# Identity turns at two seams of a one-core decoder step, a fourth early step in the MLP, and six pieces moved behind decode's last group

## The chip, the cores and the metric

The kernel runs on one core of a Trainium2 chip. The metric is the device time in microseconds of one execution. Before the change three runs took 1118.14, 1119.84 and 1120.73 us; the median is 1119.84.

## The reference

One layer of a hybrid decoder is applied to a prompt of 512 tokens and to 64 new tokens (8 sequences of 8) that have 2048 cached positions each. Width is 1024, all values are 32-bit floats.

```
h  = rmsnorm(x) ;  z = h @ w_in                 # q, k, v of two branches, gates ga, gm
att = block-sparse attention (top 3 of the blocks of 256 positions, and the own block)
ml  = chunked matrix memory with running-max stabiliser, 4 heads of 128
u   = sigmoid(ga) * (att @ w_attn_br) + sigmoid(gm) * (ml @ w_mlstm_br)
x   = x + rmsnorm(u @ w_out)
y   = x + rmsnorm(square(relu(rmsnorm(x) @ w_up)) @ w_down)      # w_up 1024 x 4096
```

For the new tokens the attention reads all cached keys of their sequence (for block means and scores) and the cached values, through a page table: 64 MB in pages of 128 positions.

## The kernel before

Every engine has one instruction stream, written out by hand; semaphores order them, and each engine works strictly in its own order. The stages are: first norm and turn of x, projection with the matrix memory beside it, prompt attention, decode attention, merge, MLP.

**Matmuls.** 32-bit products are made of three matmuls with reduced operands: each operand is split in a high part (ScalarE, `w_high`, L336) and a low part (VectorE, `w_low`, L347). One step is 128 rows of a weight chunk of 512 columns; it is loaded by SP into one of four slots, split, and used by TensorE. A slot can be filled again when TensorE has used it. In `features_chunk` (L497) a step is 24 matmuls: eight PSUM banks, three matmuls each; even banks hold the first half (288) of the 576 tokens, odd banks the second. With `early` the first `EARLY` = 3 steps do their even banks first, then a callback, then their odd banks, and then the other steps follow. So TensorE can work while the last token tiles aren't ready.

**First seam.** `first_pe` waits for the identity matrix (semaphore `masked`, made by POOL), then turns the normed tiles 0 to 3 with eight transposes each (`first_turn`, L571). ScalarE copies the high part out (L596), VectorE the low part (L607). Tile 4 (the 64 new tokens) is turned inside the first `features_chunk`, after its first step.

**Second seam.** After the merge's last matmuls (`kept_tiles`, L435 and L442), VectorE forms the new x (L2377), its norm (L552), and TensorE turns each tile (`mixed_turn`, L2226). Tile 3's turn stands at the end of `pe_merge`. The MLP's first chunk then does three steps' even banks, `last_turn` (tile 4's turn, and a wait until banks 1, 3, 5 and 7 are free), and goes on. ScalarE and VectorE split three steps (`AHEAD` = 3) at e == 2 in `act_merge` and `dve_merge`, the others in `act_mlp` and `dve_mlp`.

**Decode.** The work on the cache is 32 groups of four pages, taken in slots. In slot s TensorE forms the scores of group s-1 (L1928), turns the keys of group s (four times four transposes, L1919), turns the probabilities of group s-6 (L1944), and multiplies them with the values (L1960). Keys arrive on SP's queue in a ring of two groups, values on POOL's queue in another. At two places in each slot, ahead of the last two key turns and behind the values, TensorE takes half pieces of other work: gates (L890) and branches (L906). `pieces_in(s)` says how many whole pieces a slot holds. A piece is 12 matmuls; branch pieces are emptied by VectorE (L2185) in its next slot. In every fourth slot (s % 4 == 0) VectorE chooses the blocks of a sequence (`choose`), and ScalarE's exponentials of that sequence start in the slot after. Slots 32 to 39 have no new keys; they finish the values. All pieces together are 80 and their order is fixed; how many stand in each slot decides also in which slot the weights for them are fetched and split (`steps_in`, `fetched_in`).

Of the kernel before, what the change touches and what calls it, by code (L numbers as in the profile page):

```python
# [15 lines left out]
P = 128  # L16
D = 1024
KT = D // P
T = 512
PT = T // P  # L20
# [19 lines left out]
AHEAD = 3  # L40
# [54 lines left out]
def moba_mlstm_step(  # L95
# [57 lines left out]
    h2T = stacked("h2T", "R2", True)  # L153
# [60 lines left out]
    w_hi, w_lo, _ = pair("w", [P, NSLOT, CH], "RW")  # L214
# [4 lines left out]
    ident = sb("ident", [P, P], F32, "RC")  # L219
# [60 lines left out]
    def sem(name):  # L280
        if name not in names:
            names[name] = stack.enter_context(nc.semaphore(name))
        return names[name]
# [191 lines left out]

    EARLY = 3

    def features_chunk(eng, n, right, kt, nts=4, early=()):  # L480

        w = (w_hi, w_lo)
        slots = []
        parts = [(k, h) for h in range(2) for k in range(EARLY)] if early else []
        parts += [(k, None) for k in range(len(parts) // 2, kt)]
        for k, half in parts:
            if k == len(slots):
                slots.append(take_step(eng, n))
            j = slots[k]
            for b in range(2 * nts):  # L490
                i, h = b // 2, b % 2
                if half not in (None, h):
                    continue
                if k == 0:
                    fill(eng, n, b)
                for c, a in THREE:
                    mm = eng.matmul(ps[:, b, 0:HALFT], w[a][:, j, i * P:(i + 1) * P],  # L497
                                    right[c][:, k, h * HALFT:(h + 1) * HALFT],
                                    start=(k == 0 and (c, a) == THREE[0]),
                                    stop=(k == kt - 1 and (c, a) == THREE[-1]))  # L500
                if k == kt - 1 and b < 2 * nts - 1:
                    filled(mm, n, b)
            if half != 0:
                mm.then_inc(sem(f"w_used{j}"), 1)
            if half == 0 and k in early:
                early[k]()
# [39 lines left out]
    def norm_tile(eng, tag, e, t, src, dst, gain):  # L546
# [5 lines left out]
        eng.scalar_tensor_tensor(out=dst[0:r, t, :], in0=src[0:r, t, :], scalar=rinv[0:r, t:t + 1],  # L552
                                 in1=gain[0:r, :], op0=ALU.mult, op1=ALU.mult).then_inc(sem("normed"), 1)

    def first_pe(eng, n):

        eng.wait_ge(sem("masked"), 1)
        for t in range(PT):
            first_turn(eng, n, t)

    def first_bank(t, j):
        return (0, 1, 2, 3, 4, 5, 7, 1, 3, 5)[2 * t + j]
# [375 lines left out]
    def pieces_in(s):  # L938

        if s < VALS:  # L940
            return 2
        if s < ALL_GROUPS:
            return 2 if s % 4 == 0 else 1
        return (2, 1, 1, 2, 1, 1, 2, 0)[s - ALL_GROUPS]

    def pieces_at(g):
        return 2 - g % 2 if g < A_SLOTS else pieces_in(g - A_SLOTS)
# [1282 lines left out]
    def act_merge(eng, n):  # L2230
        for f in range(KT):
            w_high(eng, n)
            for h in range(2):
                skip(n, h, h == 1)
                eng.wait_ge(sem("u_sum"), 2 * f + h + 1)
                eng.activation(uT[0][:, f, h * HALFT:(h + 1) * HALFT], u_at(f, h), ACT.Copy, scale=0.5)\
                   .then_inc(sem("u_high"), 1)
        for _ in range(KT - AHEAD):
            w_high(eng, n)
        for k in range(KT):  # L2240
            w_high_kept(eng, n, wo_res, k)

        def squares(t, c, e):
            drain(eng, n, t, t == PT and c == 0, KT)
            if t < PT:
                eng.wait_ge(sem("mix_sq"), c * PT + e)
                eng.activation(junk2[:, 0:CH], ps[:, t, :], ACT.Square, accum_out=(sq0, sq1)[c][:, t:t + 1])\
                   .then_inc(sem("mix_sq"), 1)
            else:
                eng.activation(wide[0:NS, PT, c * CH:(c + 1) * CH], ps[LOW, PT, :], ACT.Copy)\  # L2250
                   .then_inc(sem("low_part"), 1)
                n["low_part"].add()
            n[f"free{t}"].add()

        def rms_of_mixed(e):
            t = ORDER[e]
            r = rows(t)
            squares(t, 1, e)
            if t < PT:
                eng.wait_ge(sem("mix_sqe"), 1)  # L2260
            else:
                eng.wait_ge(sem(f"free{PT}"), n[f"free{PT}"].value())
                eng.activation(junk2[0:NS, :], wide[0:NS, PT, :], ACT.Square, accum_out=sq1[0:NS, PT:TILES])\
                   .then_inc(sem("mix_sq"), 1)
            eng.wait_ge(sem("mix_sq"), PT + e + 1)
            eng.activation(rms[0:r, t:t + 1], sq1[0:r, t:t + 1], ACT.Sqrt,
                           bias=sqe[:, t:t + 1] if t < PT else eps[0:r, :], scale=1.0 / D).then_inc(sem("mix_rms"), 1)

        def rms_of_x(e):
            t = ORDER[e]  # L2270
            r = rows(t)
            eng.wait_ge(sem("x_sum"), e + 1)
            eng.activation(junk2[0:r, :], x[0:r, t, :], ACT.Square, accum_out=ssq[0:r, t:t + 1])\
               .then_inc(sem("squares"), 1)
            eng.wait_ge(sem("squares"), TILES + e + 1)
            eng.wait_ge(sem("mix_rinv"), e + 1)
            eng.activation(rms[0:r, t:t + 1], ssq[0:r, t:t + 1], ACT.Sqrt, bias=eps[0:r, :], scale=1.0 / D)\
               .then_inc(sem("rms"), 1)

        for t in range(TILES):  # L2280
            squares(t, 0, t)
        eng.wait_ge(sem("mix_sq"), PT)
        eng.activation(sqe[:, 0:PT], sq0[:, 0:PT], ACT.Identity, bias=eps[:, :], scale=1.0 / D)\
           .then_inc(sem("mix_sqe"), 1)
        for e in range(TILES):
            if e >= 1:
                rms_of_x(e - 1)
            if e >= 2:
                mixed_high(eng, n, e - 2)
            rms_of_mixed(e)  # L2290
            if e == 2:
                for _ in range(AHEAD):
                    w_high(eng, n)
        mixed_high(eng, n, TILES - 2)
        rms_of_x(TILES - 1)
        mixed_high(eng, n, TILES - 1)
# [25 lines left out]
    def dve_merge(eng, n):  # L2322
# [63 lines left out]
        for e in range(TILES):  # L2386
            if e >= 1:
                norm_tile(eng, 1, e - 1, ORDER[e - 1], x, xn, g2B)
            if e >= 2:
                mixed_low(eng, n, e - 2)  # L2390
            added(e)
            if e == 2:
                for _ in range(AHEAD):
                    w_low(eng, n)
        mixed_low(eng, n, TILES - 2)
        norm_tile(eng, 1, TILES - 1, ORDER[TILES - 1], x, xn, g2B)
# [17 lines left out]

    def pe_mlp(eng, n):
        def body(i, last):
            features_chunk(eng, n, h2T, KT, early={EARLY - 1: last_turn} if i == 0 else ())
            features_chunk(eng, n, h2T, KT)
            tokens_chunk(eng, n, hid, KT, lambda k: eng.wait_ge(sem("hid_low"), i * 16 + 2 * k + 2))
            if last:  # L2420
                for _ in kept_tiles(eng, n, hid, wd_res):
                    pass
            else:
                tokens_chunk(eng, n, hid, KT)

        def last_turn():
            mixed_turn(eng, n, TILES - 1)
            for b in (1, 3, 5, 7):
                eng.wait_ge(sem(f"free{b}"), n[f"free{b}"].value())


        for b, later in ((5, 1), (6, 0), (7, 0)):
            eng.wait_ge(sem(f"free{b}"), n[f"free{b}"].value() - later)
        mlp_passes(body)

    def act_mlp(eng, n):
        def body(i, last):
            for c in range(2):
                for _ in range(KT):
                    w_high(eng, n)  # L2440
                for b in range(9):
                    if b < 8:
                        drain(eng, n, b, b == 7)
                        eng.wait_ge(sem("hid_low"), i * 16 + 8 * c)
                        drained(eng.activation(rl[:, b, :], ps[:, b, 0:HALFT], ACT.Relu), n, b)
                    if b >= 1:
                        u = b - 1
                        eng.wait_ge(sem("hid_sq"), i * 16 + 8 * c + u + 1)
                        k = 4 * c + u // 2
                        eng.activation(hid[0][:, k, (u % 2) * HALFT:(u % 2 + 1) * HALFT], rl[:, u, :], ACT.Copy)\  # L2450
                           .then_inc(sem("hid_high"), 1)
            if last:
                return
            for c in range(2):
                for _ in range(KT):
                    w_high(eng, n)
                for t in range(TILES):
                    skip(n, t, t == TILES - 1)
# [27 lines left out]
    def dve_mlp(eng, n):  # L2486
        def body(i, last):
            for c in range(2):
                for _ in range(KT):
                    w_low(eng, n)  # L2490
                for b in range(9):
                    if b < 8:
# [181 lines left out]
```

## Time and profile before

| what | value |
|---|---|
| median of three runs | 1119.84 us |
| profiled execution | 1118.83 us |
| its span, first to last instruction | 1117.2 us |
| TensorE busy | 1066.3 us (95%) |
| VectorE / ScalarE / POOL busy | 563.8 / 449.5 / 126.6 us |
| mean granted TensorE clock | 0.989 |

PE is TensorE's matmul side, PEld its weight loads, DVE is VectorE, ACT ScalarE, POOL GpSimd, SP the engine that issues loads; ACTq is ScalarE's queue. Transposes appear as MATMUL with `ident`. L571 is line 571 of the kernel; a line can be that of a helper. "[1.96 <-DVE xn L552]" says that the engine was idle for 1.96 us before the instruction and what released it.

### The profile page before, as it was taken

What the parts mean: (1) busy time and instruction counts of PE and PEld (TensorE: products, weight loads), DVE (VectorE), ACT (ScalarE), POOL (GpSimd) and SP (SyncE); (2) the same over time, 40 slices, a digit from 0 to 9 for tenths busy, and PEclk for the clock granted to TensorE, in tenths of its full rate; (3) what the DMA queues carried; (4) which work ended last, traced back from release to release, by engine and by line L of the source; (5) the groups of instructions that cost most, each with busy time, mean ns of one, the idle gap of its engine ahead of it and who ended that gap; (6) DMA issues with size and microseconds to landing.
All of it is one profiled execution on the core that took longest, in us unless ns stands there. A gap on an engine that the chain in (4) does not pass through costs nothing.

```text
span 1117.2 us, 20695 instructions
## 1 busy us (share of the span) xinstructions
PE 1066.3 (95%) x7593; PEld 910.2 (81%) x7593; DVE 563.8 (50%) x1227; ACT 449.5 (40%) x1023; POOL 126.6 (11%) x227
## 2 busy tenths in 40 slices
PE   4999999999999999999988998999999999999997
PEld 4977877887777777767768886998899899889985
DVE  5254534545675655655644747443344334433456
ACT  5253233324554555555543355342144113322441
POOL 4003110221001033323331100100000000000000
PEclk8999999999999999999999999999999999999999
DMA  6432216234136799989974440223222222222222
GB/s 214 117 86 57 67 48 142 57 85 124 48 96 188 202 326 309 322 308 339 321 218 132 150 134 29 95 76 94 84 77 86 85 76 86 80 81 85 77 85 85
DMA packets 93716, 150.02 MB, mean 134 GB/s; under 512 B 9377, under 2 KB 39590, under 8 KB 93622
## 3 DMA queue, kind: packets, MB, share of 16 engines
q1 hardware_dynamic: 75040, 103.83, 30.6%
q0 software_dynamic: 11968, 39.85, 10.6%
q10 hardware_dynamic: 6614, 5.06, 1.6%
q8 instruction: 61, 1.00, 0.4%
q14 instruction: 33, 0.27, 0.1%
HBM read 141.62 MB, written 7.10 MB: 133 GB/s over the span
## 4 chain that ended last, share of the span: by engine, by line
PE 78%; DVE 9%; issue 4%; ACT 3%; DMA 3%; SPq 1%; POOLq 1%; ACTq 1%; POOL 0%; DVEq 0%
PE ps L462 27%; PE ps L497 19%; PE ps L890 7%; PE ps L470 4%; PE ps L1919 4%; PE ps L906 3%; PE ps L435 2%; DMA kring<-in_cache_k_dram 2%; PE ps L1928 1%; PE ps L1960 1%; DVE xn L552 1%; PE ps L1054 1%; PE ps L1074 1%; PE ps L1064 1%; ACT sP L2036 1%
## 5 line engine op out<-in xcount | busy, mean ns | idle before, releaser
L347 DVE TENSOR_TENSOR w<-w,w 128x512 fp32r<-128x512 f32 (+1 forms) x240 | 168.0, 706 | 305.6 <-ACT w L336 301.0
L336 ACT ACTIVATE w<-w 128x512 fp32r<-128x512 f32 (+1 forms) x240 | 145.2, 613 | 337.7 <-PE ps L470 172.4
L497 PE MATMUL ps<-h2T,w 128*128 128x288 f32 x1536 | 210.0, 297 | 4.3 <-DVE wide L2529 1.7
L497 PEld LDWEIGHTS ps<-h2T,w 128*128 128x128 f32 x1536 | 207.1, 189 | 7.2 <-DVE wide L2529 2.4
L462 PE MATMUL ps<-w,hid 128*128 128x512 f32 x672 | 161.6, 389 | 0.0
L462 PEld LDWEIGHTS ps<-w,hid 128*128 128x128 f32 x672 | 125.9, 188 | 26.0
L462 PE MATMUL ps<-w,hT 128*128 128x512 f32 x576 | 145.3, 401 | 1.4 <-ACT ri L811 1.4
L462 PEld LDWEIGHTS ps<-w,hT 128*128 128x128 f32 x576 | 106.0, 190 | 26.6 <-issue 4.9
L890 PE MATMUL ps<-hT,w 128*128 128x288 f32 x768 | 124.2, 305 | 0.0
L890 PEld LDWEIGHTS ps<-hT,w 128*128 128x128 f32 x768 | 104.7, 188 | 11.3 <-issue 10.6
L1886 POOL DMA_DIRECT2D vring<-in_cache_v_dram x128 | 68.8, 538 | 180.1 <-issue 180.1
L1919 PEld LDWEIGHTS ps<-ident,kring 128*128 128x128 f32 x512 | 56.6, 140 | 36.5 <-DMA kring<-in_cache_k_dram 18.5
L2090 DVE COPY kT<-ps 128x512 f32<-128x512 f32 x64 | 44.1, 689 | 79.3 <-PE ps L1919 79.1
L1919 PE MATMUL ps<-ident,kring 128*128 128x128 f32 x512 | 68.5, 277 | 8.4 <-DMA kring<-in_cache_k_dram 4.6
L2020 ACT ACTIVATE kT<-ps 128x512 f32<-128x512 f32 x64 | 38.2, 597 | 37.8 <-PE ps L1919 37.7
L2036 ACT ACTIVATE sP<-sS,sbias 128x256 f32<-128x256 f32 x64 | 31.7, 498 | 26.2 <-DVE sbias L2122 26.2
L1960 PE MATMUL ps<-vring,sPT 128*32 128x128 f32 x1024 | 34.8, 276 | 6.4 <-DMA vring<-in_cache_v_dram 6.4
L497 PE MATMUL ps<-hT,w 128*128 128x288 f32 x240 | 35.0, 310 | 3.5 <-DVE w L347 3.5
L497 PEld LDWEIGHTS ps<-hT,w 128*128 128x128 f32 x240 | 34.5, 201 | 3.8 <-issue 3.7
L1960 PEld LDWEIGHTS ps<-vring,sPT 128*32 128x32 f32 x1024 | 26.0, 109 | 12.0 <-DMA vring<-in_cache_v_dram 7.1
L470 PE MATMUL ps<-w,hid 128*128 128x512 f32 x112 | 34.5, 389 | 0.0
L1928 PE MATMUL ps<-kT,qb 128*32 128x512 f32 x256 | 34.1, 605 | 0.0
(354 smaller groups left out, 1279.1 us busy)
## 6 DMA issues: line engine op xcount, KB each, us to landing
kring<-in_cache_k_dram SPq DMA_DIRECT2D x128, 256.0 KB, 4.1
vring<-in_cache_v_dram POOLq DMA_DIRECT2D x128, 256.0 KB, 4.5
w<-in_w_in_dram SPq DMA_DIRECT2D x88, 256.0 KB, 2.9
w<-in_w_up_dram SPq DMA_DIRECT2D x64, 256.0 KB, 2.8
w<-in_w_down_dram SPq DMA_DIRECT2D x64, 256.0 KB, 2.8
w<-in_w_out_dram SPq DMA_DIRECT2D x16, 256.0 KB, 3.0
x<-in_x_prompt_dram SPq DMA_DIRECT2D x4, 512.0 KB, 6.9
out_dram<-sC ACTq DMA_DIRECT2D x1, 2048.0 KB
```

The costliest lines, as they stand in the source:

```text
L336: eng.activation(spread(w_hi, n, j, width), together(w32, n, j, width), ACT.Copy)\
L347: eng.tensor_tensor(spread(w_lo, n, j, width), together(w32, n, j, width), spread(w_hi, n, j, width).bitcast(F32), ALU.subtract).then_inc( ...
L462: mm = eng.matmul(ps[:, t, :], left[a][:, k, prompt_cols(t)], w[b][:, j, :], start=(k == 0 and (a, b) == THREE[0]), stop=(k == kt - 1 and ...
L470: mm = eng.matmul(ps[:, PT, :], left[2][:, k, T:NT + NS], w[b][:, j, :], start=(k == 0 and b == 0), stop=(k == kt - 1 and b == 1))
L497: mm = eng.matmul(ps[:, b, 0:HALFT], w[a][:, j, i * P:(i + 1) * P], right[c][:, k, h * HALFT:(h + 1) * HALFT], start=(k == 0 and (c, a) == ...
L890: mm = eng.matmul(ps[:, h, 0:HALFT], w[a][:, slots[part], (k % 4) * P:(k % 4 + 1) * P], hT[c][:, k, h * HALFT:(h + 1) * HALFT], start=(k = ...
L1886: eng.dma_start(ring[:, 4 * (g % 2) + j, :], flat[bass.ds(page, 1), :, :].rearrange("a p n -> (a p) n"))\
L1919: mm = eng.transpose(ps[:, 2 + h % 2, j * P:(j + 1) * P], kring[:, (m % 2) * 4 + j, h * P:(h + 1) * P], ident[:, :])
L1928: mm = eng.matmul(ps[32 * h:32 * h + 32, 4, :], qb[:, (m // GROUPS) % 2, h, :], kT[:, h, :], start=True, stop=True)
L1960: mm = eng.matmul(ps[32 * h:32 * h + 32, 6, 0:P], sPT[m % 2][:, j, 32 * h:32 * h + 32], vring[:, 4 * (m % 2) + j, h * P:(h + 1) * P], star ...
L2036: eng.activation(sP[m % 2][:, c], sS[:, g * CH:(g + 1) * CH][:, c], ACT.Exp, bias=sbias[:, 2 * g + k:2 * g + k + 1], scale=SC, accum_out=s ...
L2090: eng.tensor_copy(kT[:, h, :], ps[:, 3, :]).then_inc(sem("p_kT_dve"), 1)
```

## The change

Five things are done. A helper `keep_busy` issues transposes of the identity into a PSUM bank that nobody reads at that time. `first_pe` calls it with 28 turns before tile 0, 5 after tiles 0, 1 and 2, and 16 after tile 3. The MLP's first chunk has four early steps instead of three, and ScalarE and VectorE split the fourth with the three others. `last_turn` gets 8 identity turns before tile 4's turn, and 12 between the waits for its banks. In decode the slots 8, 12, ... 28 hold one piece instead of two, and the slots from 32 on hold (3,2,2,3,2,2,2,0) instead of (2,1,1,2,1,1,2,0).

```diff
-    EARLY = 3
+    EARLY, EARLY_UP = 3, 4
...
-        parts = [(k, h) for h in range(2) for k in range(EARLY)] if early else []
+        parts = [(k, h) for h in range(2) for k in range(max(early) + 1)] if early else []
...
+    def keep_busy(eng, b, times):
+
+        for _ in range(times):
+            eng.transpose(ps[:, b, 0:P], ident[:, :], ident[:, :])
+
     def first_pe(eng, n):
 
         eng.wait_ge(sem("masked"), 1)
+        keep_busy(eng, 6, 28)
         for t in range(PT):
             first_turn(eng, n, t)
+            keep_busy(eng, 6, 5 if t < PT - 1 else 16)
...
         if s < ALL_GROUPS:
-            return 2 if s % 4 == 0 else 1
-        return (2, 1, 1, 2, 1, 1, 2, 0)[s - ALL_GROUPS]
+            return 1
+        return (3, 2, 2, 3, 2, 2, 2, 0)[s - ALL_GROUPS]
...
             if e == 2:
-                for _ in range(AHEAD):
+                for _ in range(EARLY_UP):
                     w_high(eng, n)
...
             if e == 2:
-                for _ in range(AHEAD):
+                for _ in range(EARLY_UP):
                     w_low(eng, n)
...
-            features_chunk(eng, n, h2T, KT, early={EARLY - 1: last_turn} if i == 0 else ())
+            features_chunk(eng, n, h2T, KT, early={EARLY_UP - 1: last_turn} if i == 0 else ())
...
         def last_turn():
+            keep_busy(eng, 7, 8)
             mixed_turn(eng, n, TILES - 1)
-            for b in (1, 3, 5, 7):
+            for b in (5, 1):
+                eng.wait_ge(sem(f"free{b}"), n[f"free{b}"].value())
+            keep_busy(eng, 1, 12)
+            for b in (3, 7):
                 eng.wait_ge(sem(f"free{b}"), n[f"free{b}"].value())
...
-                for _ in range(KT):
+                for _ in range(KT - (EARLY_UP - AHEAD if i == c == 0 else 0)):
                     w_high(eng, n)
...
-                for _ in range(KT):
+                for _ in range(KT - (EARLY_UP - AHEAD if i == c == 0 else 0)):
                     w_low(eng, n)
```

## Rows read from the trace of the kernel before

**Rows 1.** The page, part 1: busy time, share of the span, instructions.
```profile
PE 1066.3 (95%) x7593; PEld 910.2 (81%) x7593; DVE 563.8 (50%) x1227; ACT 449.5 (40%) x1023; POOL 126.6 (11%) x227
```

**Rows 2.** Windows: stretch and length; busy (instructions) by engine; clock, DMA, GB/s.
```profile
20.84:27.67 6.83, 6.83 (x33) 6.44 (x32) 2.87 (x7) 0.77 (x3) 1.47 (x2) 0.50 0.85 253
...
567.70:604.85 37.15, 29.91 (x365) 25.93 (x365) 13.21 (x38) 11.44 (x32) 10.75 (x20) 0.95 0.63 181
696.68:703.50 6.82, 4.94 (x24) 4.78 (x25) 2.19 (x6) 1.79 (x4) 4.90 (x2) 0.50 0.19 77
398.13:567.70 169.57, 163.93 (x1909) 127.07 (x1909) 99.93 (x251) 94.82 (x244) 51.59 (x96) 1.00 0.93 318
```

**Rows 3.** Timeline of PE, 0 to 75 us: start, length, instruction, idle before.
```profile
15.58 1.09 PE L571 MATMUL ps<-ident,xn 128*128 128x128 f32 x8 [0.86 <-DVE xn L552]
20.15 2.62 PE L497 MATMUL ps<-hT,w 128*128 128x288 f32 x12 [3.47 <-DVE w L347]
...
23.75 32.39 PE L497 MATMUL ps<-hT,w 128*128 128x288 f32 x228
```

**Rows 4.** Line 571's turns, 11.0 to 11.5 and 16.0 to 16.5 us: min/median/max ns.
```profile
L571 PE MATMUL ps<-ident,xn x4: 421/421/421, 10.8 to 11.4; 128*128 128x128 f32 x4
...
L571 PE MATMUL ps<-ident,xn x7: 272/272/273, 15.7 to 16.4; 128*128 128x128 f32 x7
```

**Rows 5.** Timeline of POOL, ACT's queue and DVE, 0 to 32 us.
```profile
3.68 0.29 POOL L646 TENSOR_SCALAR_AFFINE_SELECT ident<-ident 128x128 f32<-128x128 f32 x1 [0.23 <-POOL vm L624]
...
24.80 5.18 ACTq L2607 DMA_DIRECT2D snn<-in_state_n_dram  x1
...
30.82 1.29 DVE L347 TENSOR_TENSOR w<-w,w 128x512 fp32r<-128x512 f32 x2 [5.56 <-ACT w L336]
```

**Rows 6.** Timeline of PE, 655 to 726 us.
```profile
687.80 1.09 PE L2226 MATMUL ps<-ident,xn 128*128 128x128 f32 x8 [1.96 <-DVE xn L552]
689.15 4.97 PE L497 MATMUL ps<-h2T,w 128*128 128x288 f32 x36 [0.26 <-issue]
696.86 1.11 PE L2226 MATMUL ps<-ident,xn 64*128 64x64 f32 x8 [2.74 <-DVE xn L552]
699.68 26.55 PE L497 MATMUL ps<-h2T,w 128*128 128x288 f32 x180 [1.70 <-DVE h2T L2315]
```

**Rows 7.** Timelines of DVE and POOL, 655 to 730 us.
```profile
678.25 1.89 DVE L347 TENSOR_TENSOR w<-w,w 128x512 fp32r<-128x512 f32 x3
...
683.43 1.28 DVE L2377 SCALAR_TENSOR_TENSOR x<-wide,rinv,x 128x1024 f32<-128x1024 f32 x1
...
698.46 4.37 POOL L2592 MEMSET wide<- 128x5120 f32 x1 [0.82 <-ACT h2T L2303]
```

**Rows 8.** Timeline of PE, decode slots 24 to 28.
```profile
512.00 1.07 PE L1928 MATMUL ps<-kT,qb 128*32 128x512 f32 x8
...
520.07 1.06 PE L1928 MATMUL ps<-kT,qb 128*32 128x512 f32 x8
...
523.76 1.09 PE L1919 MATMUL ps<-ident,kring 128*128 128x128 f32 x8 [0.36 <-ACT kT L2020]
...
539.61 1.06 PE L1928 MATMUL ps<-kT,qb 128*32 128x512 f32 x8
```

**Rows 9.** Timelines of DVE and ACT, 505 to 525 us.
```profile
517.45 0.69 DVE L2090 COPY kT<-ps 128x512 f32<-128x512 f32 x1 [1.32 <-PE ps L1919]
...
521.07 0.51 ACT L2036 ACTIVATE sP<-sS,sbias 128x256 f32<-128x256 f32 x1 [3.00 <-DVE sbias L2122]
```

**Rows 10.** Waits of PE, 567.7 to 604.9 us: total, times, longest.
```profile
PE ps L1960 <- DMA vring<-in_cache_v_dram: 6.4, 3, 3.6
```

**Rows 11.** Timeline of PE behind the last group.
```profile
567.70 1.06 PE L1928 MATMUL ps<-kT,qb 128*32 128x512 f32 x8
...
574.99 1.03 PE L906 MATMUL ps<-mlT,w 128*128 128x288 f32 x6 [0.81 <-DVE sg L2185]
...
600.60 4.25 PE L906 MATMUL ps<-mlT,w 128*128 128x288 f32 x30
```

## The prediction

> **What bounds the kernel now.** I read the page first (busy shares, then the clock line), then the windows, then the order of instructions in the three places that the change touches. TensorE is busy 95% of the span [rows 1], so time comes only from its idle stretches and from stretches at the lower of its two clock levels (1.2 GHz against 2.4).
>
> At the first seam TensorE turns tile 3 at 15.58 and then idles 3.47 us until VectorE has split the first weights; the first matmuls start at 20.15 [rows 3], and soon after the granted clock is 0.50 for 6.83 us [rows 2]. From 23.75 on, 228 matmuls run with no idle in 32.39 us [rows 3]. At 0.1333 us each (3.2 us a step of 24) they need 30.4; the missing 2.0 is half of the slow time from 23.75 to 27.67. So the dip is paid in full. At the second seam it is the same after two idle stretches: 1.96 us ahead of tile 3's turn is followed by no fall, 2.74 us ahead of tile 4's turn is; TensorE then goes on at 699.68, and the clock is 0.50 until 703.50 [rows 2, 6]. In decode, slots 8 to 31 take 169.57 us, with TensorE busy 163.93 and the DMA engines at 0.93 [rows 2]: the two are nearly balanced. After the last group TensorE has gaps again, 6.4 us of them on V pages [rows 10].
>
> **First seam.** The first idle-filling turns wait only for the identity, made at 3.97 [rows 5]. Turns are 421 ns from issue to end at the start and 272 ns by 16 us, the row's figure at full clock [rows 4]; eight take 1.09 us at full clock [rows 3], so about 0.117 each, and I take 0.213 each at half. 28 of them from 4.0 end at 9.97 at the latest, where tile 0's turn starts at 9.90 now: no cost, or 0.1. Tiles 1 to 3 are given by VectorE, and 8 turns plus 5 identity turns (1.5 us at full clock) fit between them. Behind tile 3's turn (16.67) 16 more take about 1.8, to 18.3. The idle stretch before 20.15 shrinks from 3.47 to about 1.9, as long as the 1.96 that was followed by no fall. I take it that the clock holds: 6.83 / 2 = **3.4 us** gained. Late next: step 3's high part stands on ScalarE behind a DMA issue of 5.18 us (24.80 to 29.98), and its low part is done at about 31.5 [rows 5]. That issue starts about 0.9 earlier (tile 4's turn runs at full clock), so the low part comes at 30.5; TensorE wants it at 20.15 + 3 x 1.6 + 0.6 + 4.8 = 30.35. It costs 0.2. **Seam 1: -3.2** (bounds: -3.4; and +3.3, all added turns at half clock, below).
>
> The Trainium skill, TensorE: Matmul & The Clock Gate, Part 4, speaks against this: transposes don't count as PE-busy in the same way, and the full clock doesn't engage for them. The trace disagrees: from 9.90 to 14 the engine did nothing but turns, and within them they went from 421 to 272 ns [rows 4]. By the rule both seams' clock gains would be nothing.
>
> **Second seam.** Four steps' first halves instead of three: 12 matmuls, 1.6 us, move from behind the second-half point into the wait for tile 4. What is added ahead of it: a fourth split. On ScalarE 0.6 us in an idle stretch, hidden. On VectorE three low parts take 1.89 [rows 7] in a row of work without gaps (it still has none before 683.43 [rows 7]), so the fourth delays everything behind it by 0.6: the sums, norms and turns of tiles 3 and 4. Tile 3's turn goes from 687.80 to 688.4, and its idle stretch from 1.96 to 2.56. The 48 matmuls start at 689.75 and end at 696.3 (36 took 4.97 [rows 6]); 8 identity turns end at 697.2, before tile 4 is ready at 697.4. The turn takes about half of its 1.11 [rows 6], so the copies start some 0.3 earlier; 12 turns more (1.3 us) end at 699.3. Second halves then start at 699.68 + 0.6 - 0.3 = 700.0. Behind it 144 matmuls instead of 156: -1.6. The clock: from 699.68 to 703.50 half is lost, 1.9. Weights: step 4's low part waits for POOL's clearing of the sum, done at 702.8 [rows 7], and is wanted at 706.4: hidden. **Seam 2: +0.3 - 1.6 - 1.9 = -3.2** (bounds: -3.8 without the delay; +0.4 with all turns at half clock).
>
> **Decode.** A piece is 12 matmuls: 30 take 4.09 us before the next group starts [rows 11], so 1.64. Six leave slots 8, 12, ... 28; each had half ahead of the last key turns, half behind the values. Four slots now take 539.61 - 512.00 = 27.61, the first 8.07 [rows 8]. But slot 1 of each four has a wait for ScalarE's kT copy (0.36 at 523.76 [rows 8]). Behind it is a chain: last key turn of slot 0, VectorE's copy at 517.45, the choice of blocks, then ScalarE's exponentials at 521.07 after 3.00 idle [rows 9], then kT. It is about 6.4 us long and doesn't shrink. Only the half piece ahead of its start shortens the period; the half behind it turns into wait, 0.36 to about 1.2. So 6 x 0.82 = 4.9 us leave the slots, not 9.8. Of 5.64 us idle in these slots [rows 2] six kT waits make 2.2, so K pages cost some 3.5 now; with DMA at 0.93 [rows 2] there is a little room, and I take 0.6 of new waits: **-4.3**.
>
> After the last group (567.70 to 604.85, 37.15 us) TensorE is busy 29.91 at a clock of 0.95 [rows 2]: about 1.7 of the busy time is the clock. Work at full clock is 28.2; six pieces make 38.0. V pages no longer hold it up (they do now for 6.4 us, since POOL issues them at a fixed pace). But slot 32's third piece needs bank 0, which VectorE empties only after its choice of blocks, seen at 574.99 [rows 11]; TensorE gets there 0.81 (the wait now) and 0.47 (the four turns ahead of it) earlier, at 573.7, and waits 1.3: 39.3 in all, **+2.2**. The page tables, POOL's and SP's queues get no new instruction. **Decode: -4.3 + 2.2 = -2.1** (bounds: -9.8 + 0.9 = -8.9 if the chain shortens too; +2.2 if DMA takes all that the slots give).
>
> **Sum.** -3.2 - 3.2 - 2.1 = -8.5 on the profiled execution's own 1118.83 (span 1117.2), so 1110.3. The median of the runs is 1119.84, 1.0 above; against that, 1111.3.
>
> **Rivals.**
> - A fall in spite of the turns (0.24). Tile 3's wait grows to 2.56 us, between 1.96 without and 2.74 with a fall; and in the first seam 1.9 us stay idle behind turns that are lighter than matmuls. One dip more costs 1.9 to 3.4: 1113.2 to 1114.7. Both: about 1116.6 (0.06). For: no row shows how far light work counts as work. Against: 1.96 was harmless, and turns alone raised the clock once.
> - Decode is DMA's (0.10): the slots give nothing, the tail costs 2.2: 1115.6. For: 0.93 busy. Against: K waits are 3.5 of 169.57 us.
> - The chain in decode is not the limit (0.05): 4 to 6 us more, 1106 to 1107. Against: its wait shows each time.
> - Slower, one mechanism (0.05): turns never count, so the start runs at half clock. TensorE's queue is in order, and 59 added turns stand before the first matmul: 28 to 9.97, then 8 + 5, 8 + 5, 8 + 5, 8 + 16 at 0.213 end at 23.4, 3.3 later than 20.15. Both dips stay, the second seam is +0.4, decode -2.1: 1121.4. It decides if the clock is not up by tile 1's turn. Against it: 421 to 272 ns during turns alone. That the turns run but do nothing else (no rise, no delay) is the case of both dips.
>
> **Numbers.** The forecast has 0.50. A measurement of this kernel tells 0.2%, 2.2 us, from no change. Cases below 1117.6: the forecast, one dip, most of both dips, decode by DMA, the better decode, 0.84 with something kept back for what I don't see; within 0.2%: 0.10; slower 0.06. The likeliest case's own range is 1109 to 1114. The range of 1107.5 to 1116 leaves out part of the better decode, both dips and the slower case.
>
> **What would show it.** Right: clock 1.00 from 20 to 30 and from 689 to 704; matmuls at 20.15 as now, second halves near 700; kT wait of slot 1 near 1.2 in each four; slots 8 to 31 in about 165.3; from the last group's slot to the attention branch 39.3, with a wait of about 1.3 on VectorE in slot 32 and no V wait over 0.5. Wrong: a first matmul after 20.5, a granted 0.50 after 688, kT wait still 0.36, or K waits above 1 us in most fours.

## The result and the profile after

| | before | changed |
|---|---|---|
| median of 8 runs each | 1118.99 us (1114.37 to 1121.24) | 1106.82 us (1104.93 to 1114.96) |
| profiled execution / span | 1118.83 / 1117.2 us | 1112.47 / 1110.9 us |
| mean granted clock, profiled | 0.989 | 0.995 |

The ratio is 0.9897, 95% interval 0.9873 to 0.9921: 11.5 us faster, 8.8 to 14.2. The forecast was 1111.3 with a range of 1107.5 to 1116.0, so the time lies just below the range. The profiled execution of the changed kernel is the second longest of its eight: it is only 6.4 us faster than the profiled execution before.

A dip is here a stretch in which TensorE's granted clock is half, and a fall is where it begins.

TensorE at the start, timeline of the changed kernel (columns as in [rows 3]):

```profile
4.02 5.39 PE L558 MATMUL ps<-ident 128*128 128x128 f32 x28 [4.02 <-POOL ident L653]
...
16.51 1.91 PE L558 MATMUL ps<-ident 128*128 128x128 f32 x16
20.15 1.81 PE L497 MATMUL ps<-hT,w 128*128 128x288 f32 x12 [1.73 <-DVE w L347]
...
32.20 22.66 PE L497 MATMUL ps<-hT,w 128*128 128x288 f32 x168 [1.45 <-DVE w L347]
56.30 3.20 PE L462 MATMUL ps<-w,hT 128*128 128x512 f32 x12 [1.43 <-ACT ri L818]
```

The matmuls start at 20.15 as in [rows 3], the 12 first take 1.81 us instead of 2.62, but a wait of 1.45 us has come in at 30.75, ahead of step 3. The row at 56.30 is the start of the first tokens chunk (L462), the stage behind these matmuls. ScalarE's queue and VectorE behind it, the changed kernel's answer to [rows 5]:

```profile
22.70 0.84 ACTq L2617 DMA_DIRECT2D sC<-in_state_C_dram  x1
23.58 7.04 ACTq L2618 DMA_DIRECT2D snn<-in_state_n_dram  x1
30.73 2.19 ACT L336 ACTIVATE w<-w 128x512 fp32r<-128x512 f32 x4 [7.68 <-issue]
...
31.46 2.50 DVE L347 TENSOR_TENSOR w<-w,w 128x512 fp32r<-128x512 f32 x4 [7.24 <-ACT w L336]
```

The issue of `state_n` that took 5.18 us takes 7.04: begun 1.2 earlier, ended 0.6 later. The windows (columns as in [rows 2]; the same stretch, then a dip in the matrix memory stage, slots 8 to 31, and the stretch behind the last group):

```profile
20.84:27.67 6.83, 6.83 (x56) 6.60 (x55) 2.87 (x7) 0.66 (x3) 1.48 (x2) 1.00 0.92 277
134.60:141.40 6.80, 6.80 (x21) 5.41 (x20) 1.55 (x3) 0.00 (x0) 0.00 (x0) 0.51 0.15 39
399.28:561.32 162.04, 154.51 (x1838) 117.61 (x1837) 95.51 (x243) 93.41 (x240) 51.60 (x96) 1.00 0.96 326
561.32:601.40 40.08, 37.69 (x437) 33.94 (x436) 17.21 (x46) 13.51 (x36) 10.75 (x20) 1.00 0.65 194
```

Half clock is gone at the start; a half-clock stretch of 6.8 us stands in the matrix memory stage, where the kernel before had one of 3.4 and where a second execution of the changed kernel (a1_again, below) had none. The slots take 162.04 us instead of 169.57 [rows 2], the stretch behind the last group (the tail) 40.08 instead of 37.15. Tails are told from here on up to the first row of the attention branch: 40.07 instead of 37.02. The second seam, against [rows 6]:

```profile
685.11 1.09 PE L2233 MATMUL ps<-ident,xn 128*128 128x128 f32 x8 [2.53 <-DVE xn L552]
686.47 6.56 PE L497 MATMUL ps<-h2T,w 128*128 128x288 f32 x48 [0.27 <-issue]
692.87 1.04 PE L558 MATMUL ps<-ident 128*128 128x128 f32 x8
694.17 0.71 PE L2233 MATMUL ps<-ident,xn 64*128 64x64 f32 x8 [0.27 <-DVE xn L552]
694.82 1.53 PE L558 MATMUL ps<-ident 128*128 128x128 f32 x12
696.61 18.63 PE L497 MATMUL ps<-h2T,w 128*128 128x288 f32 x138 [0.26 <-issue]
```

Tile 3's wait is 2.53 as forecast (2.56); the others are nearly gone. In the slots, scores (L1935) and waits of slots 24 to 26, against [rows 8]:

```profile
507.22 1.07 PE L1935 MATMUL ps<-kT,qb 128*32 128x512 f32 x8
513.73 1.06 PE L1935 MATMUL ps<-kT,qb 128*32 128x512 f32 x8
514.99 1.09 PE L1926 MATMUL ps<-ident,kring 128*128 128x128 f32 x8 [0.19 <-DMA kring<-in_cache_k_dram]
517.91 1.09 PE L1926 MATMUL ps<-ident,kring 128*128 128x128 f32 x8 [0.59 <-ACT kT L2027]
521.28 1.07 PE L1935 MATMUL ps<-kT,qb 128*32 128x512 f32 x8
```

The start of slot 26 in the kernel before:

```profile
527.14 1.06 PE L1928 MATMUL ps<-kT,qb 128*32 128x512 f32 x8
```

Slots 24 and 25 together take 14.06 us (521.28 - 507.22) instead of 15.14 (527.14 - 512.00). The wait for kT is 0.59 here, and 0.88 at the most in this trace; the forecast was near 1.2 in each four.

### The profile page after: what moved, and what is told of

It is laid out like the page before. It is cut to its first block, busy times and chain, and to the rows that moved or that the text cites. A ratio compares the mean times of both kernels' runs of the same rounds, so it can differ in the third digit from the quotient of the medians.

```text
span 1110.9 us, 20855 instructions
## 1 busy us (share of the span) xinstructions
PE 1070.9 (96%) x7672; PEld 913.8 (82%) x7672; DVE 563.3 (51%) x1227; ACT 449.3 (40%) x1023; POOL 126.6 (11%) x227
## 4 chain that ended last, share of the span: by engine, by line
PE 78%; DVE 9%; DMA 4%; issue 3%; ACT 3%; SPq 1%; ACTq 1%; POOLq 0%; POOL 0%; DVEq 0%
PE ps L462 27%; PE ps L497 18%; PE ps L897 7%; PE ps L470 4%; PE ps L1926 4%; PE ps L913 3%; DMA kring<-in_cache_k_dram 3%; PE ps L435 2%; PE ps L1967 2%; PE ps L1935 2%; DVE xn L552 1%; PE ps L1061 1%; PE ps L1081 1%; DMA vring<-in_cache_v_dram 1%; PE ps L1951 1%
## 5 line engine op out<-in xcount | busy, mean ns | idle before, releaser
L462 PE MATMUL ps<-w,hid 128*128 128x512 f32 x672 | 161.6, 389 | 0.0
L462 PE MATMUL ps<-w,hT 128*128 128x512 f32 x576 | 146.2, 403 | 1.4 <-ACT ri L818 1.4
L462 PEld LDWEIGHTS ps<-w,hid 128*128 128x128 f32 x672 | 125.9, 188 | 26.1
L462 PEld LDWEIGHTS ps<-w,hT 128*128 128x128 f32 x576 | 106.5, 191 | 26.7 <-issue 4.9
L470 PE MATMUL ps<-w,hid 128*128 128x512 f32 x112 | 34.5, 389 | 0.0
L1935 PE MATMUL ps<-kT,qb 128*32 128x512 f32 x256 | 34.1, 605 | 0.0
L2461 ACT ACTIVATE hid<-rl 128x288 fp32r<-128x288 f32 x64 | 28.4, 444 | 8.1 <-DVE rl L2506 7.1
```

Source lines behind the costliest of these rows:

```text
L462: mm = eng.matmul(ps[:, t, :], left[a][:, k, prompt_cols(t)], w[b][:, j, :], start=(k == 0 and (a, b) == THREE[0]), stop=(k == kt - 1 and ...
L470: mm = eng.matmul(ps[:, PT, :], left[2][:, k, T:NT + NS], w[b][:, j, :], start=(k == 0 and b == 0), stop=(k == kt - 1 and b == 1))
L1935: mm = eng.matmul(ps[32 * h:32 * h + 32, 4, :], qb[:, (m // GROUPS) % 2, h, :], kT[:, h, :], start=True, stop=True)
```

## The experiments

Each kernel was timed beside the kernel before. Half clock is (1 - mean granted clock) x 2 x span, a mean over all runs of the kernel: half clock counts 0.5 in the granted clock, so this is the length of all stretches at half clock. In the traces 4.5 to 7.5 us of it stand at the end of the span, behind TensorE's last matmul, off the path. The runs of one kernel (5 to 12 each, 8 at first, and 29, 12 and 11 of the kernel before) lie up to 14 us apart, with a standard deviation of 1 to 4 us, so means of half clock and the traces' stretches carry more than one median. The a, b and c kernels were each timed in a set of their own; where means of different sets are compared, the gain over the set's own mean before is the fairer number. It is 10.6 us for the changed kernel both times (the mean before was 1118.8 beside its first set).

| kernel | median us | ratio to before (95%) | mean us | half clock us |
|---|---|---|---|---|
| before, three sets | 1120.01, 1118.80, 1119.24 | | 1119.2, 1118.3, 1119.2 | 24.8, 24.0, 25.0 |
| changed, first | 1106.82 | 0.9897 (0.9873-0.9921) | 1108.2 | 9.7 |
| a1_again | 1108.41 | 0.9910 (0.9875-0.9944) | 1108.7 | 9.6 |
| a2_start_only | 1116.73 | 0.9987 (0.9966-1.0008) | 1117.5 | 19.7 |
| a3_decode_only | 1112.70 | 0.9952 (0.9931-0.9972) | 1113.4 | 21.3 |
| a4_mlp_only | 1116.09 | 0.9981 (0.9960-1.0002) | 1116.7 | 21.0 |
| b1_no_turns | 1112.13 | 0.9947 (0.9928-0.9967) | 1112.1 | 21.6 |
| b2_snn_first | 1109.68 | 0.9920 (0.9898-0.9942) | 1109.0 | 11.5 |
| b3_total_first | 1107.39 | 0.9902 (0.9880-0.9924) | 1106.9 | 7.5 |
| b4_later4 | 1108.34 | 0.9915 (0.9891-0.9938) | 1108.5 | 11.4 |
| c1_all_four | 1104.54 | 0.9883 (0.9843-0.9922) | 1105.6 | 7.4 |
| c2_three_of_four | 1106.54 | 0.9885 (0.9849-0.9921) | 1106.0 | 8.5 |
| c3_mlp_no_turns | 1107.65 | 0.9900 (0.9865-0.9935) | 1107.6 | 10.0 |
| c4_only16 | 1108.94 | 0.9911 (0.9876-0.9947) | 1109.4 | 9.2 |

**The changed kernel again (a1_again),** no edit. 

> The changed kernel once more, unedited, for a second trace. Theory A (the two traces differ by the three parts, and the changed kernel's profiled execution paid 6.83 us at half clock in the matrix memory stage, which is chance): the time falls by 9 to 12 us against the kernel before, and a trace without that dip has decode starting about 3 us earlier than the first one (347.87). Theory B (the 6.4 us between the two profiled executions is all there is): 6 to 7 us, and the spread of the earlier runs is noise of both kernels alike.

Theory A, in its mean: 10.6 us below the mean before. This trace has no dip in the matrix memory stage, and decode starts at 343.06 instead of 347.87, 4.8 us earlier where theory A had 3. Its slots took 163.66 us and its tail 39.39. But it has a dip at the second seam, behind tile 3's wait, where the first trace had none:

```profile
679.83 1.09 PE L2233 MATMUL ps<-ident,xn 128*128 128x128 f32 x8 [2.54 <-DVE xn L552]
681.19 8.06 PE L497 MATMUL ps<-h2T,w 128*128 128x288 f32 x48 [0.27 <-issue]
```

and its window, at half clock:

```profile
681.00:684.50 3.50, 3.31 (x14) 3.34 (x15) 1.92 (x3) 2.53 (x5) 0.00 (x0) 0.51 0.00 0
```

The 48 matmuls take 8.06 instead of 6.56 us.

**Start turns only (a2_start_only).**

```diff
-    EARLY, EARLY_UP = 3, 4
+    EARLY, EARLY_UP = 3, 3
...
-            return 1
-        return (3, 2, 2, 3, 2, 2, 2, 0)[s - ALL_GROUPS]
+            return 2 if s % 4 == 0 else 1
+        return (2, 1, 1, 2, 1, 1, 2, 0)[s - ALL_GROUPS]
...
-            keep_busy(eng, 7, 8)
...
-            keep_busy(eng, 1, 12)
```

> Only the turns at the start, all else as before. Theory A (the clock is held, but step 3's weights stand behind the blocked DMA issue on ScalarE's queue): first tokens chunk starts 1.3 us earlier (57.56 before), clock 1.00 from 20 to 28 us, whole time -1 to -2 us. Theory B, the prediction's own step: -3.2 us. Theory C (turns don't count as work): dip stays, 0 to +0.5.

Theory A. The queue was blocked for 6.38 us, the wait ahead of step 3 was 0.80, and the first tokens chunk began at 55.52. Four traces without start turns have it at 57.56, 58.30, 55.94 and 57.98 (dips of 6.8, 10.2, 3.4 and 10.2 us), so their mean is 57.4. The mean time is 1.7 us below before, half clock 5.1 us. The interval of the ratio holds 1, here and in a4_mlp_only: by the times alone neither part is told from no change, and their sizes rest on the traces.

**Moved pieces only (a3_decode_only).**

```diff
-    EARLY, EARLY_UP = 3, 4
+    EARLY, EARLY_UP = 3, 3
...
-        keep_busy(eng, 6, 28)
...
-            keep_busy(eng, 6, 5 if t < PT - 1 else 16)
...
-            keep_busy(eng, 7, 8)
...
-            keep_busy(eng, 1, 12)
```

> Only the six pieces moved. Theory A (the period of four slots is set by the chain from slot 0's last key turn, and K waits lie inside the time that the chain takes): slots 8 to 31 take 161 to 163 us instead of 169.57, slot 0 and 1 of each four together 14.0 to 14.1, the tail is about 3 us longer than 37.15; whole time -3.5 to -5.5 us. Theory B, the prediction's: 165.3 and 39.3, whole time -2.1. Theory C (DMA takes it all): slots unchanged, +2.

Theory A: 159.46 us for slots 8 to 31, tail 39.56, the pairs of slot 0 and 1 at 14.05, 14.06, 14.05, 14.17, 14.05, 14.05. The mean is 5.8 us below before. It is the largest part.

**Second seam only (a4_mlp_only).**

```diff
-            return 1
-        return (3, 2, 2, 3, 2, 2, 2, 0)[s - ALL_GROUPS]
+            return 2 if s % 4 == 0 else 1
+        return (2, 1, 1, 2, 1, 1, 2, 0)[s - ALL_GROUPS]
...
-        keep_busy(eng, 6, 28)
...
-            keep_busy(eng, 6, 5 if t < PT - 1 else 16)
```

> Only the second seam: four early steps and the 20 turns. Theory A (as predicted): from the end of the merge's last matmuls to the second tokens stage 3.1 to 3.3 us less, no half clock, whole time -3.2. Theory B (the longer wait ahead of tile 3's turn, 2.5 us, lets the clock fall in some executions): -1 to -2 in the median, with a wide spread.

Between the two. From the merge's second matmul stage (its first row at L435) to the MLP's first tokens stage (its first row at L462) it took 88.64 us, against 90.87, 91.26 and 91.28 in three traces with three early steps; a half-clock stretch of 3.4 us stood behind tile 3's wait. The mean is 2.5 us below before.

**No turns at all (b1_no_turns).**

```diff
-        keep_busy(eng, 6, 28)
...
-            keep_busy(eng, 6, 5 if t < PT - 1 else 16)
...
-            keep_busy(eng, 7, 8)
...
-            keep_busy(eng, 1, 12)
```

> The changed kernel without its 83 identity turns: fourth early step and moved pieces stay. Half clock is told as (1 - mean granted clock) x 2 x span, a mean over all runs: 24.8 us before, 9.7 changed, of which about 5 stand at the very end. Theory A (the turns hold the clock at both seams): about 9 us more at half clock than the changed kernel, 3.5 to 4.5 us slower than it, the first seam's dip back. Theory B (the fourth step and the fuller tail alone close the gaps at the second seam, the turns there do nothing): only the first seam's 6 us come back, 1.5 to 2.5 us slower. Theory C (turns do nothing anywhere): same time as the changed kernel.

12 us more at half clock and 3.9 us slower in the mean than the changed kernel's first set (over its own set's mean before it gains 6.2 us, the changed kernel 10.6), as theory A has it in size. The trace's dip at the start was 10.2 us long. But at the second seam it had one dip, behind tile 3's wait as in a1, and none ahead of the second halves, as theory B has it in place.

**The small state load first (b2_snn_first).**

```diff
+            eng.dma_start(snn[:, :], state_n...).then_inc(sem("d_n_in"), 16)
             eng.dma_start(sC[:, :, :], state_C...).then_inc(sem("d_C_in"), 16)
-            eng.dma_start(snn[:, :], state_n...).then_inc(sem("d_n_in"), 16)
```

> The changed kernel with the two state loads on ScalarE's queue in the other order: the small one (state_n) is issued before the large one (state_C). Theory A (the second issue blocks ScalarE for 5 to 7 us because the queue is still full of the large load's descriptors): ScalarE gets to step 3's split near 24.5 instead of 30.7, the wait of 0.6 to 1.5 us at about 32 is gone, first tokens chunk near 54.5 to 54.9, whole time -0.6 to -1.4 us. Theory B (the block is the small load's own strided pattern): 5 us of it stay, nothing changes.

Theory A for the queue; ScalarE's queue and its splits in this kernel:

```profile
22.70 0.28 ACTq L2617 DMA_DIRECT2D snn<-in_state_n_dram  x1
23.30 0.89 ACTq L2618 DMA_DIRECT2D sC<-in_state_C_dram  x1
24.30 0.63 ACT L336 ACTIVATE w<-w 128x512 fp32r<-128x512 f32 x1 [1.03 <-issue]
```

The small load is issued in 0.28 us and nothing blocks; the wait on step 3 is gone. The first tokens chunk starts at 54.65 (56.30 in the changed kernel's first trace; its second also has 54.65, but its matmuls began 0.5 us earlier). From the first matmul on it is 34.5 us here, and 34.2 in c1 and c2, which have the same order of loads; it is 35.0 to 36.2 in the six traces with all start turns and the old order. In the times of the runs the gain isn't seen: the mean is 1109.0, 9.3 us below its own mean before where the changed kernel has 10.6, with more half clock than the first set.

**Sum and reciprocal ahead of the kT copy (b3_total_first).**

```diff
+            if s % GROUPS == 0 and s >= GROUPS + EXPS - 1 and (s - GROUPS) // GROUPS - 1 < B:
+                total((s - GROUPS) // GROUPS - 1)
             if s < ALL_GROUPS:
                 keys(s, 3)
             if s % GROUPS == 0 and s >= GROUPS:
-                if s >= GROUPS + EXPS - 1 and (s - GROUPS) // GROUPS - 1 < B:
-                    total((s - GROUPS) // GROUPS - 1)
```

> The changed kernel with VectorE's sum and reciprocal of the exponentials (0.31 us of queue time) ahead of the last kT copy in every fourth slot. Theory A (slot 1 ends when the chain over the choice of blocks does): slots 0 and 1 of a four together 13.7 instead of 14.05, slots 8 to 31 2 us less where K pages don't intervene. Theory B (K pages set the period): no change, the K waits grow by as much as the kT waits fall.

Theory A: the pairs are 13.72, 13.87, 13.72, 14.63, 13.94 and 13.73 us, the least 0.33 less than the least of the six traces with the changed slots and the old order so far (14.04 to 14.05), and the kT wait fell from 0.87 to 0.54 at the most. Slots 8 to 31 took 158.54 us, the least of all traces, with 2.3 us of waits for K pages. VectorE's queue in slot 16, the sum and reciprocal ahead of the copy:

```profile
452.42 0.16 DVE L2138 TENSOR_REDUCE srt<-srs 128x1 f32<-128x9 f32 x1
452.61 0.16 DVE L2139 RECIPROCAL sri<-srt 128x1 f32<-128x1 f32 x1
452.86 0.69 DVE L2097 COPY kT<-ps 128x512 f32<-128x512 f32 x1
...
455.93 0.23 DVE L2129 TENSOR_SCALAR sbias<-sneg,snx 128x8 f32<-128x8 f32 x1
```

**The fourth split later (b4_later4).**

```diff
             if e == 2:
-                for _ in range(EARLY_UP):
+                for _ in range(AHEAD):
                     w_high(eng, n)
+            if e == 3:
+                w_high(eng, n)
```

and the same for `w_low`. 

> The changed kernel with the fourth step's split behind tile 3's sum (e == 3), where ScalarE and VectorE idle, instead of with the three others at e == 2. Theory A (the fourth low part delays the chain of sums and norms by 0.6): TensorE's wait ahead of tile 3's turn falls from 2.5 to 1.9 us, second halves start 0.6 earlier, and the clock falls there less often: whole time -0.6 to -1.5. Theory B (the norms' chain absorbs it): no change.

The wait fell from 2.53 to 1.94 us, but the trace had a dip of 3.4 us behind it all the same: a wait of 1.94 us can be followed by a fall too. The times show nothing beyond their spread.

**All four edits (c1_all_four), and three (c2_three_of_four).** c2 is b2, b3 and b4 together; c1 adds:

```diff
+        eng.wait_ge(sem("free5"), n["free5"].value())
+        keep_busy(eng, 5, 14)
         mixed_turn(eng, n, TILES - 2)
```

> The changed kernel with state_n loaded first, the sum and reciprocal ahead of the kT copy, the fourth split at e == 3, and 14 identity turns more ahead of tile 3's turn at the second seam. Theory A (each removes what its trace showed): against the changed kernel -0.6 to -1.4 for the blocked queue, -1.5 to -2 in the slots, -0.6 for the split, -0.5 to -1 for the falls at tile 3's wait: 3 to 4.5 us faster than it, half clock 6 to 8 us in the mean. Theory B (they hide one another, above all the slots behind K pages): 1 to 2 us faster.

> The same without the 14 added turns ahead of tile 3's turn. Theory A (a fall at this wait costs something): half clock 2 us more in the mean than with them, time 0.5 to 1 more. Theory B (TensorE has slack behind it, the fall is free): same time, more half clock.

c1 is the fastest kernel of the study: 1104.54, mean 1105.6, 2.6 and 3.0 below the two means of the changed kernel; its interval overlaps theirs. That is the lower edge of its theory A, but not by theory A's sum: slots 8 to 31 took 161.37 us in c1 and 161.18 in c2, no less than the mean of 161.3 with the old order. The shorter pairs were eaten by K pages (5.5 and 5.3 us of waits, 2.3 in b3), as theory B has it. What its trace shows instead is the first seam (34.2 us to the first tokens chunk) and the second (87.17 us to the MLP's tokens stage, against a mean of 88.4). Its pairs are 13.72 five times out of six, and tile 3's wait is 0.40 with no dip:

```profile
674.37 1.69 PE L558 MATMUL ps<-ident 128*128 128x128 f32 x14
676.46 1.09 PE L2235 MATMUL ps<-ident,xn 128*128 128x128 f32 x8 [0.40 <-DVE xn L552]
677.81 6.56 PE L497 MATMUL ps<-h2T,w 128*128 128x288 f32 x48 [0.26 <-issue]
```

c2 had the dip (7.96 us for the 48 matmuls) and its second halves began 42.76 us after the merge's second matmul stage, against 41.70 in c1; 0.4 us more in the mean, with 1.1 us more half clock, less than its theory A has. That the added turns gain is shown in one trace of each, not in the times.

**No turns at the second seam (c3_mlp_no_turns).**

```diff
-            keep_busy(eng, 7, 8)
...
-            keep_busy(eng, 1, 12)
```

> The changed kernel without its 20 turns at the second seam; start turns and the fourth step stay. Theory A (the fourth step alone leaves too little idle for a second fall, as in the trace without any turns): same half clock, 9 to 11 us in the mean, same time within 1. Theory B (the turns hold the clock here): 3 us or more at half clock more, 1.5 us slower, falls right ahead of the second halves.

Theory A: half clock 10.0, mean 1107.6. The fourth step does the work there; the 20 turns do none that can be measured.

**Only 16 turns at the start (c4_only16).**

```diff
-        keep_busy(eng, 6, 28)
...
-            keep_busy(eng, 6, 5 if t < PT - 1 else 16)
+            if t == PT - 1:
+                keep_busy(eng, 6, 16)
```

> The changed kernel with only the 16 turns behind tile 3 at the start: the 28 before tile 0 and the 5 behind each of tiles 0 to 2 are gone. Theory A (it is the shortened idle stretch ahead of the first matmuls that holds the clock): same half clock and same time as the changed kernel, tile 0 turned at half clock, no dip at 20 us. Theory B (all turns are needed): a dip in the trace at 20 us, 3 to 5 us more at half clock, 1.5 to 2.5 us slower.

Theory A for the clock: half clock 9.2, no dip at 20 us in the trace. The 24 turns of tiles 0 to 2 take 5.26 us in one row, nearly all of them at the 421 ns that [rows 4] has at half clock, and the matmuls start at 20.18 all the same. The mean is 1109.4, 0.8 to 1.2 above the changed kernel's two, within their errors.

## Why the prediction was right and wrong

The direction held, and the time fell 0.7 us below the range. One term, the decode slots, was forecast too small because a step of its mechanism was wrong; at the first seam a second step was wrong the other way, and at the second seam the turns had no part. Against each term stand means over traces: those with the part and those without it.

- **Base.** The reference of 1119.84 was the median of three runs; of eight it is 1118.99.
- **First seam, forecast -3.2.** With all the start turns and the old order of the loads, the first tokens chunk came 35.6 us after the first matmul (six traces), without turns 37.3 us (four): -1.7. No trace with start turns has a dip there, all four without them have one, and the 28 turns delayed nothing. In c4 the 16 behind tile 3, which shorten the idle stretch from 3.47 to 1.72 us, are enough. The step that failed is "that issue starts about 0.9 earlier, so the low part comes at 30.5": the forecast took the 5.18 us of the issue as a fixed length, its cost as 0.2. Begun at 23.1 to 23.6 instead of 24.8 to 25.4, it took 6.0 to 7.4 us, and step 3 was 0.4 to 1.8 us late. Its end, at 29.3 to 31.0 in the traces with turns and 30.0 to 31.2 in those without, moved by 0.5 us in the mean. b2 shows that the order of the two loads is the cause; what the issue waits for, room in the queue perhaps, no run shows. With the other order (b2, c1, c2) the chunk comes after 34.3 us: the clock gives 3.0, close to the forecast's 3.4, and the held issue takes 1.3 of it back.
- **Second seam, forecast -3.2.** -2.7 in the traces (91.1 in three to 88.4 in eight). Tile 3's wait grew as computed, and the rival "a fall in spite of the turns" was real here: of eight traces with a wait of 2.53 to 2.58 us six fell there. It costs little (the seam takes 87.78 us in the two traces without a fall, 87.95 to 89.00 in the six with one), since the 48 matmuls at half clock partly replace the wait for tile 4. The forecast's reason, that the turns hold the clock, isn't borne out: without them (c3) half clock is 10.0 us against 9.7 and 9.6, where 3 us more were expected of it. So the size was met in part for another reason, the fourth early step; that is luck.
- **Decode slots, forecast -4.3: the term that was mis-sized.** -7.5 (168.8 in three traces, 161.3 in eight). The mechanism, a chain from slot 0's last key turn to slot 1's kT copy, is shown by the constancy of the pair of slots: 15.14 at the least in before's order, 14.05 in the changed one, 13.72 when 0.31 us is taken out of the chain. But the step "it is about 6.4 us long and doesn't shrink" failed. ScalarE's timeline has in it, behind the exponentials and ahead of the scores' copy, the activation of the piece's gate. Before:

```profile
522.26 0.18 ACT L2040 ACTIVATION_READ_ACCUMULATOR spow<-sown,snx 128x1 f32 x1
522.36 0.39 ACT L991 ACTIVATE sg<-ps 128x288 f32<-128x288 f32 x1
522.65 0.58 ACT L2026 ACTIVATE sS<-ps 128x512 f32<-128x512 f32 x1
```

and after, at the same place of the order:

```profile
516.70 0.19 ACT L2047 ACTIVATION_READ_ACCUMULATOR spow<-sown,snx 128x1 f32 x1
516.79 0.57 ACT L2033 ACTIVATE sS<-ps 128x512 f32<-128x512 f32 x1
```

With the piece its gate activation left slot 1: 0.3 us (from the first exponential to this copy, behind which the kT copy stands, 1.58 us before, 1.28 after). The pair of slots lost 15.14 - 14.05 = 1.09 instead of 0.82: 1.6 us in six. The kT wait agrees: 0.36 + 0.82 - 0.30 gives 0.88, and the most in a trace is 0.86 to 0.88 in seven of the eight (0.49 in b2), not the forecast's 1.2. This is read from the traces; no run moved that activation alone. The rest of the gap is K waits. I added 0.6, but where a K wait falls into the chain's time it costs nothing (the forecast's 2.2 us of kT waits and 3.5 of K waits before are 1.7 and 3.9 in its trace): slot 9 of the first trace waits 1.03 for K pages, and its pair still takes 14.08. Beyond chain and PE work the slots lost 2.7 to 3.9 us in the three traces of before's order (over 6 x 27.61), and 0.3 to 4.5 (over 6 x 26.53) in the eight of the changed order, 1.1 less in the mean. Why they lost less, with the same K pages in less time, stays open.
- **Tail, forecast +2.2.** +2.7 (36.8 to 39.5). The wait for bank 0 in slot 32 was 1.38 (1.3 forecast). Waits for V pages were left in five of the eight traces, 0.69 the longest in the first and 1.76 in c4, where the forecast had none over 0.5.
- **The rule on transposes.** That the full clock doesn't engage for turns is against the nine traces here that begin with the 28 identity turns and nothing else: from 4.02 on they take 421 ns each from issue to end, the last of them 272 to 273. The 28 took from 4.69 us (a2) to 6.05 (b4, where nearly all are at 421 ns). 6.05 / 28 = 0.216 bears out the 0.213 a turn at half clock that the forecast took without showing a row for it. That turns also keep the clock shows at the first seam: without any turns (b1) 12 us of half clock come back, without those of the second seam alone (c3) none.

The terms as measured in traces give -1.7 - 2.7 - 7.5 + 2.7 = -9.2; the three parts run alone, in their means, -1.7 - 2.5 - 5.8 = -10.0; the changed kernel -11.5 and -10.1 by its two ratios. These agree within their errors. That the sum in traces is close to the forecast's -8.5 is luck too: the slots gave 3.2 more than forecast, the first seam 1.5, the second 0.5 and the tail 0.5 less. The time also lies in the range of a rival (1106 to 1107, chance 0.05), but its mechanism, that the chain isn't the limit, isn't what happened: the kT wait stood on.

The clock's part is about 7.5 us by estimate, half of the 24.8 - 9.7 us of half clock that went. The traces show where. At the start the dips are 7.7 us long in the mean without turns and none with them. At the second seam they are 6.8 us long in the three traces with three early steps, and 2.6 in the mean of the eight with four and a wait of 2.5 us for tile 3. Behind the last group two of the three traces with the old order of pieces have a dip of 3.4 us, none of the eleven with the new one. And in the matrix memory stage, which no part of the change touches, three of the four traces without start turns have one of 3.4 us, and of the ten with them only the first (6.8) and c4 (twice 3.4). Whether that follows from the start turns or is chance, no experiment shows.

## What to carry to other kernels

When a piece of work is taken out of a slot, follow every instruction that it has on the other engines too; here the small activation on ScalarE stood in the chain that set the period, and the least of a repeating period over several traces shows such a chain better than any wait. A long DMA issue may stand for "until" and not "for": here one that began 1.2 us earlier ended 0.6 later. And when two kernels differ by chance events of some us each, one profile per kernel misleads: the mean clock of all runs gave the size of the clock's part.

## What was not expected of the hardware

The length of an idle stretch alone didn't decide whether the clock fell behind it: ahead of tile 3's turn, 1.93 to 1.96 us of idle were followed by a fall in two traces of five (b4 and c2), 2.53 to 2.58 us in six of eight. At the first seam, behind the same 3.47 us of idle, the dip was 3.4, 6.8 or 10.2 us long. A second DMA issue on an engine's queue, behind a strided load of 2 MB, kept the engine for 5.2 to 7.4 us; in the other order the two issues took 0.28 and 0.84 to 0.89 us.
